# A transposed copy of x at the opening, and gate and up weights in one array laid out by chunk and row

## The reference

```
x = x + 0.5 * SwiGLU_1(rmsnorm(x, ffn1_norm))
x = x + token_mixing(rmsnorm(x, mix_norm), ...)     # three attentions on one projection, gated, then w_out
x = x + 0.5 * SwiGLU_2(rmsnorm(x, ffn2_norm))
rmsnorm(x, g) = x * rsqrt(mean(x * x) + 1e-6) * g
swiglu(x)     = (silu(x @ w_gate) * (x @ w_up)) @ w_down      # 1024 -> 2816 -> 1024
```

## Time and profile before

| | |
|---|---|
| time, median of 3 runs | 1138.39 us (1137.74 to 1138.44) |
| time of the profiled execution | 1138.71 us |
| its span, first to last instruction | 1136.9 us |
| TensorE busy | 1133.1 us of the span |
| VectorE / ScalarE / GpSimd busy | 770.4 / 630.6 / 70.3 us |
| read from memory | 205.29 MB, 181 GB/s over the span |

### The profile page before, as it was taken

The page is one execution under the profiler, slowest core; times in us unless marked ns, Lnnn a source line. Parts: engine busy times, 40 slices in busy tenths (PEclk is TensorE's granted clock), DMA queues, the critical chain, the costliest instruction groups (busy, mean ns, idle before and its releaser), DMA issues.

```text
span 1136.9 us, 16092 instructions
## 1 busy us (share of the span) xinstructions
PE 1133.1 (100%) x5975; PEld 966.9 (85%) x5975; DVE 770.4 (68%) x1055; ACT 630.6 (55%) x941; POOL 70.3 (6%) x79
## 2 busy tenths in 40 slices
PE   9999999999999999999999999999999999999999
PEld 7888888888888888888888888888887888888887
DVE  5766666868768676655766856678676695766655
ACT  6644445666674564544564544466766745544542
POOL 3020000202000000000020200002110000000000
PEclk9999999999999999999999999999999999999999
DMA  9956654545544666656566555636445445656521
GB/s 324 319 175 198 187 192 140 185 136 198 148 148 152 219 223 187 193 177 219 172 169 228 185 185 186 200 98 220 148 163 172 182 154 183 222 185 202 193 86 37
DMA packets 138828, 207.34 MB, mean 182 GB/s; under 512 B 6898, under 2 KB 99876, under 8 KB 138756
## 3 DMA queue, kind: packets, MB, share of 16 engines
q1 hardware_dynamic: 137364, 205.02, 55.1%
q0 software_dynamic: 752, 0.79, 0.8%
q10 hardware_dynamic: 640, 0.55, 0.2%
HBM read 205.29 MB, written 1.05 MB: 181 GB/s over the span
## 4 chain that ended last, share of the span: by engine, by line
PE 100%; DVE 0%; issue 0%; POOL 0%; DVEq 0%; POOLq 0%
PE bank L560 28%; PE bank L530 17%; PE bank L534 17%; PE bank L533 17%; PE bank L564 15%; PE bank L546 1%; PE bank L859 1%; PE bank L849 1%; PE bank L830 1%; PE bank L668 1%; PE bank L848 1%; PE bank L877 1%; PE bank L569 0%; PE bank L738 0%; PE bank L735 0%; PE bank L732 0%
## 5 line engine op out<-in xcount | busy, mean ns | idle before, releaser
L1300 DVE TENSOR_TENSOR w_low<-raw,w_high 128x1024 fp32r<-128x1024 f32 x388 | 464.2, 1232 | 281.4 <-ACT w_high L1016 280.8
L1016 ACT ACTIVATE w_high<-raw 128x1024 fp32r<-128x1024 f32 x387 | 393.5, 1055 | 317.8 <-PE bank L564 173.5
L560 PE MATMUL bank<-xT,w_high 128*128 128x512 f32 x1388 | 331.6, 390 | 0.1
L560 PEld LDWEIGHTS bank<-xT,w_high 128*128 128x128 f32 x1388 | 257.0, 188 | 51.2 <-DVE xT L1318 0.2
L564 PEld LDWEIGHTS bank<-xT,w_low 128*128 128x128 f32 x1408 | 175.7, 191 | 3.6
L564 PE MATMUL bank<-xT,w_low 128*128 128x256 f32 x1408 | 178.6, 283 | 0.0
L530 PE MATMUL bank<-w_high,xT 128*128 128x512 f32 (+1 forms) x440 | 171.3, 389 | 0.0
L534 PE MATMUL bank<-w_low,xT 128*128 128x512 f32 (+1 forms) x440 | 168.2, 382 | 0.0
L533 PE MATMUL bank<-w_high,xT 128*128 128x512 f32 (+1 forms) x440 | 168.1, 382 | 0.0
L530 PE MATMUL bank<-w_high,oT_high 128*128 128x512 f32 x418 | 162.6, 389 | 0.0
L534 PE MATMUL bank<-w_low,oT_high 128*128 128x512 f32 x418 | 162.2, 388 | 0.0
(11 more groups left out here) (146 smaller groups left out, 771.5 us busy)
## 6 DMA issues: line engine op xcount, KB each, us to landing
raw<-in_w_in SPq DMA_DIRECT2D x92, 512.0 KB, 4.6
raw<-in_ffn_w_down SPq DMA_DIRECT2D x88, 512.0 KB, 4.3
raw<-in_ffn_w_gate SPq DMA_DIRECT2D x86, 512.0 KB, 4.1
raw<-in_ffn_w_up SPq DMA_DIRECT2D x86, 512.0 KB, 5.0
raw<-in_w_out SPq DMA_DIRECT2D x16, 512.0 KB, 4.4
raw<-in_w_branch_c SPq DMA_DIRECT2D x8, 512.0 KB, 4.0
raw<-in_w_branch_a SPq DMA_DIRECT2D x4, 512.0 KB, 4.1
raw<-in_w_branch_b SPq DMA_DIRECT2D x4, 512.0 KB, 6.0
```

The lines of the kernel that those rows point to most:

```text
L560: return nc.tensor.matmul(bank[b0 + n][:, :], w_high[:, slot, column(k, n)], xT[:, k], start=k == 0, stop=full_last and k == KB - 1)
L1016: act.activation(w_high[:, slot], raw[:, in_slot, (p % 2) * 1024:(p % 2) * 1024 + 1024], ACT.Copy).then_inc(sem["high_ready"], 1)
L1300: dve.tensor_tensor(w_low[:, slot], raw[:, FILL_SLOT[p // 2], (p % 2) * 1024:(p % 2) * 1024 + 1024], w_high[:, slot].bitcast(F32), ALU.sub ...
```

## The change

Three things are changed together.

- The host hands in `x_turned`, x transposed to 1024x256. Five transfers bring it to SBUF in blocks of 128 features (1, 1, 2, 2, 2 blocks; rows of 1 KB per block). ACT and DVE make the high and low parts of the blocks from it, and the 16 transposes of x go. The squares are taken on ACT from `x_turned` (two times 128x1024), DVE sums them over the eight blocks with one `tensor_reduce` that reads 128x2048 elements in steps of 1 KB, and two float32 matmuls with a column of ones (`sum_squares`) sum over the partitions; ACT copies the two sums out, POOL's `norm` follows as before. `turn_row` moves from after 16 wide matmuls of chunk 2 to after 24 wide and 8 narrow ones; `sum_squares` stands where `cold_row` stood. x itself is loaded later, on POOL's queue, after the fourth hidden chunk; `trig` and the small parameters are loaded after the second one. In the cold start, the squares stand before `high(0, 4)` on ACT, and on DVE the reduce stands before `low(0, 4)`, and `low(0, 7)` before the scaling by the row.
- The gains come as one array `gains` with features in the partitions; the gain transposes (L978, L723) and the copies after them go. POOL scales the diff_subln column.
- Gate and up weights come as one array, laid out by chunk, half, row and block: a row of a block is 2 KB (256 gate and 256 up columns), and a fill's two transfers take two blocks each, 4 KB in one piece. For the first pairs each transfer is one block of 256 KB.

The warm-up becomes one run of 11 matmuls on a tile of ones. Pair 0 is cut by block: DVE copies the high half of block 0 itself, ACT that of block 1.

```diff
-            load_x(0)
-            load_x(1)
-            first_rows(sp, 1, fill_landed[FILL_SLOT[0]])
-            load_x(2)
-            first_rows(sp, 2, first_landed[2])
-            first_rows(sp, 3, fill_landed[FILL_SLOT[1]])
+            load_x_turned(0)
+            load_x_turned(1)
+            load_x_turned(2)
+            first_rows(sp, 2, 2, fill_landed[FILL_SLOT[0]])
+            load_x_turned(3)
+            first_rows(sp, 4, 2, third_landed)
+            load_x_turned(4)
+            first_rows(sp, 6, 2, fill_landed[FILL_SLOT[1]])
...
+                    v = slot.rearrange("p (k c) -> p k c", k=4)
+                    for k in (0, 2):
+                        yield v[:, k:k + 2], w[bass.ds(layer, 1), bass.ds(c, 1), k0 // 4, :, k:k + 2].rearrange("o n p k c -> p (o n k) c")
...
+            def sum_squares():
+                pe.wait_ge(sem["up_summed"], 1)
+                pe.wait_ge(block_squares_summed, 1)
+                for half in range(HALVES):
+                    last = nc.tensor.matmul(bank[4][:, half:half + 1], block_sums[:, half * P:half * P + P], ones[:, 0:1].bitcast(F32),
+                                            start=True, stop=True)
+                last.then_inc(squares_summed, 1)
...
                     if opens and not turned:
-                        cold_row()
+                        sum_squares()
                     gate_up_wide(layer, p + 2, 2, done + 1, i * 12)
                     gate_up_narrow(layer, p, 0, done + 1, i * 12).then_inc(sem["pair_used"], 1)
+                    if opens and not turned:
+                        turn_row(0, 1, 4)
...
-            warm(WARM_FIRST)
+            warm(WARM)
             pe.wait_ge(ident_ready, 1)
-            pe.wait_ge(first_gains_loaded, 16)
-            nc.tensor.transpose(bank[3][:, 0:16], gain_rows[0:16, :], ident[0:16, 0:16]).then_inc(first_gains_turned, 1)
-            warm(WARM_SECOND)
...
+                act.wait_ge(gains_loaded, 16)
+                act.wait_ge(x_turned_landed[0], 16)
+                block(0).then_inc(block0_high, 1)
+                act.wait_ge(x_turned_landed[1], 16)
+                block(1).then_inc(sem["blocks_high"], 1)
+                high(0, 0)
+                for p in range(1, 4):
+                    act.wait_ge(x_turned_landed[p + 1], 16)
+                    block(2 * p)
+                    block(2 * p + 1).then_inc(sem["blocks_high"], 1)
+                    high(0, p)
+                for first in (0, D):
+                    last = act.activation(x_squares[:, first:first + D], x_turned[:, first:first + D], ACT.Square)
+                last.then_inc(block_squares_ready, 1)
                 high(0, 4)
-                act.wait_ge(x_loaded[2], 16 * HALVES)
-                squares()
...
+                dve.wait_ge(half_landed[0], 16)
+                dve.tensor_copy(w_high[:, slot, 0:512], raw[:, in_slot, 0:512]).then_inc(half_high, 1)
+                dve.drain()
+                half_of_low(slice(0, 512)).then_inc(half_low, 1)
...
                 p = 4
+                dve.wait_ge(block_squares_ready, 1)
+                dve.tensor_reduce(block_sums, x_squares.rearrange("p (k s) -> p s k", k=KB), axis=AXIS_X, op=ALU.add).then_inc(block_squares_summed, 1)
                 low(0, p)
                 low(0, p + 1)
                 sum_gate(0, 1)
                 sum_up(0, 1)
                 low(0, p + 2)
+                low(0, p + 3)
                 dve.wait_ge(sem["row_ready"], 1)
```

More of the change, by code:

```diff
@@ L220, in build, with first_rows @@
         block = ctx.enter_context(nc.Block())
[L222 to L227, removed]
+        def first_rows(engine, k0, nk, landed):
+            v = raw[:, FILL_SLOT[k0 // 4]].rearrange("p (k c) -> p k c", k=4)
+            for k in range(k0, k0 + nk):
+                engine.dma_start(v[:, k % 4], a["ffn1_gate_up"][0, 0, k // 4, :, k % 4]).then_inc(landed, 16)
         def qk_blocks(first, count):
@@ L667, in warm @@
                 for _ in range(count):
-                    nc.tensor.matmul(bank[7][:, :].rearrange("p (a b) -> p a b", a=4), zero[:, :],
-                                     zero[:, :].unsqueeze(1).to_broadcast([P, 4, P]), start=True, stop=True)
+                    nc.tensor.matmul(bank[7][:, :].rearrange("p (a b) -> p a b", a=4), ones[:, :],
+                                     ones[:, :].unsqueeze(1).to_broadcast([P, 4, P]), start=True, stop=True)
             def cold_chunk():
                 b0 = inner_bank(1)
[L675 to L680, removed]
                 full, high_part, low_part = inner_parts(PAIR_SLOT[0], b0)
-                pe.wait_ge(sem["blocks_high"], 1)
+                pe.wait_ge(block0_high, 1)
                 pe.wait_ge(half_high, 1)
@@ L685, in cold_chunk @@
                     high_part(0, n, w_high, True)
+                pe.wait_ge(half_low, 1)
+                for n in range(4):
+                    high_part(0, n)
+                pe.wait_ge(block0_low, 1)
+                for n in range(4):
+                    low_part(0, n)
+                pe.wait_ge(sem["blocks_high"], 1)
                 pe.wait_ge(sem["high_ready"], value("high_ready", 0, 1))
@@ L1121, in ffn_chunks @@
                 if not cold:
[L1122 removed]
+                    act.activation(sink_exp_of[0][:, 0:1], ones[:, 0:1].bitcast(F32), ACT.Silu)
                     act.drain()
@@ L1642, in _ @@
             dve.sem_inc(sem["low_ready"], CREDIT["low_ready"])
-            dve.wait_ge(first_gains_ready, 1)
-            dve.wait_ge(lam_init_ready, 1)
             for layer in range(DEPTH):
                 if layer == 0:
-                    for p in range(4):
-                        blocks_low(layer, ST_FFN1, p // 2, G_FFN1, (p % 2,))
-                        low(layer, p)
+                    cold_pairs()
                 else:
@@ L1680, in rotary_constants, with gate_up_rows, gain_columns @@
     return np.ascontiguousarray(table.reshape(2, HALVES, P, DH).transpose(2, 0, 1, 3).astype(np.float32))
+def gate_up_rows(gate, up):
+    both = np.stack([gate, up], axis=2).reshape(DEPTH, 2, 4, P, 2, CHUNKS, FC)
+    return np.ascontiguousarray(both.transpose(0, 5, 1, 3, 2, 4, 6).reshape(DEPTH, CHUNKS, 2, P, 4, 2 * FC))
+def gain_columns(inputs):
+    columns = [inputs[name].reshape(DEPTH, KB, P).transpose(2, 0, 1) for name in ("ffn1_norm", "mix_norm", "ffn2_norm")]
+    columns.append(inputs["diff_subln"].reshape(DEPTH, 1, P).transpose(2, 0, 1))
+    columns.append(np.broadcast_to(np.asarray(LAM_INIT, np.float32).reshape(1, DEPTH, 1), (P, DEPTH, 1)))
+    return np.ascontiguousarray(np.concatenate(columns, axis=2).astype(np.float32))
 def kernel(**inputs):
```

172 lines of the change are left out of this document (87 added, 85 removed).

## The result

| | before | after |
|---|---|---|
| median | 1138.38 us (1137.58 to 1138.78, 22 runs) | 1139.70 us (1139.19 to 1140.14, 22 runs) |
| profiled execution, span | 1138.71, 1136.9 us | 1139.23, 1137.4 us |

The changed kernel takes 1.0012 times as long, with an interval of 1.0007 to 1.0018: 1.3 us more.

A forecast was written before the change was run, and what follows sets the result against it. TensorE's own list was taken to bound the kernel (busy 1133.1 of 1136.9 us). An earlier start and dropped transposes, less new waits, gave -1.25 us: 1138.39 - 1.25 = 1137.1 us, range 1135.2 to 1139.4.

The forecast's parts named there:

- the reduce reads 2048 elements in steps of 1 KB [...] I take 2.3: DVE's sum of squares ahead of `sum_up`, priced at 2.3 us from contiguous rows of 1.06 ns an element.
- The other end, 4.6: Upper price in us kept for DVE's reduce, twice the contiguous 2.3.
- the strided reduce: Rival: DVE's reduce ahead of `sum_up` dearer than 2.3 us; at twice that 1139.4 us; chance 0.10 for over 1.5 times.
- the predicted 31.35: Start of the down product in chunk 1, in us, against 32.59 before: 1.25 us earlier.
- No PE wait afterwards: Behind the first down matmul, near 31.4 us, TensorE would wait for nothing more.
- The start of the work: First real matmul, pair 0, would come at 5.95 us instead of 8.13, range 5.3 to 6.2.
- The low clock: Pair 0: matmuls from 5.95 to 6.8 us run at half rate, costing 0.43 us.
- The cover is spent by the move of the row: First down product: moved `turn_row` leaves fewer matmuls over the 5.85 us chain to `hidden_low`; TensorE waits 1.2 us.
- To spare 1.2: Before `turn_row`: ACT's copy and POOL's part hidden by 2.8 us of matmuls, with 1.2 us to spare.
- the landing at 12.92: Last weights of chunk 1, predicted to be issued at 6.44 us and landed 6.5 later, at 12.95.
- the layout's price of nothing: Larger weight rows claimed to be worth nothing past the opening, as no PE wait is put down to a transfer.
- the later loads of x and the constants: Loads of x, `trig` and parameters on POOL's queue, claimed to cost nothing; about 6.5 us once if cover were missing.

The follow-up runs named there:

- `layout_only`: Kernel before with only the gate and up weights read from the new array, opening as it was: 1138.71 us, 1.0002 of before.
- the five executions above: Single profiled executions of the changed kernel and four variants of it; last weights of chunk 1 landed at 12.92 to 13.45 us, executions took 1139.23 to 1139.76 us.
- `warm3`: Changed kernel with 3 warm-up matmuls in place of 11: 1139.62 us, 1.0010 of before.
- `row_early`: Changed kernel with `turn_row` ahead of the eight narrow matmuls, right behind the third group of wide ones: 1139.70 us, 1.0013 of before.
- `row_filled`: Changed kernel with high 8, high 9 (ACT) and low 8, low 9 (DVE) ahead of the row; strided reduce stays: 1138.80 us, 1.0004 of before.
- `tree_filled`: `row_filled` with three contiguous additions in place of the strided reduce as well: 1137.56 us, 0.9992 of before.
- `old_fills`: Changed kernel with weight fills past the first four pairs read from the old arrays in rows of 1 KB: 1139.56 us, 1.0010 of before.

## Why the prediction was wrong

**The step that failed** is "the reduce reads 2048 elements in steps of 1 KB [...] I take 2.3". It measured 3.90, 1.7 times the contiguous price. The other end, 4.6, was kept, and the rival "the strided reduce" gave 1139.4 for it: the right mechanism with the right place, at a chance of 0.10. That 1139.4 lies so near the measured 1139.70 is luck, though: by the rival's own sum the measured 3.90 makes 1138.7. I chose by the nearest row, which was a row of another access; nearest in kind it wasn't. The Trainium skill, page "SBUF — State Buffer", section "Door 1: The DMA port swizzle", says that each access that crosses to a new 16-byte line pays a penalty. The runs agree: 3.90 in steps of 1 KB, 2.29 in order.

**From the predicted 31.35 for the first down matmul to 32.96,** step by step:

| stretch | predicted | measured | difference |
|---|---|---|---|
| to the reduce (weights land 12.95; squares) | 16.05 | 15.93 | -0.12 |
| the reduce | 2.3 | 3.90 | +1.60 |
| from its end to `sum_squares` | 3.65 | 3.53 | -0.12 |
| sums, 16 matmuls, `turn_row` | 3.45 | 3.73 | +0.28 |
| from the turn to the end of `hidden_low` | 5.85 | 5.82 | -0.03 |

So the chain was right but for one term; the 0.28 is what a restart costs (the sums 0.61 and the first wide eight 1.95, for 0.43 and 1.84). At 31.35 the first down matmul would have ended at 31.85, against 33.21 before: a gain of 1.36, where I had 1.25 by comparing weight loads, of which before's ran ahead of its matmul. 1.61 later that is a loss of 0.25, as chunk 3's start shows (0.27).

**"No PE wait afterwards" was wrong.** DVE's backlog reaches `sum_up` of chunk 2 and costs 0.21 more. I had followed each wait to the next one on TensorE and not what DVE still owed. Together +0.48, the profiled pair's difference. The median lies another 0.8 off: I took it to be 0.3 below the profiled execution, as before's is, and it is 0.5 above. Both halves come from times of one execution that I took for fixed. The start at 8.13 is 7.46 in `layout_only`. And the chain now begins with a landing, which took 6.50 to 6.87 us from its issue in the five executions above. Of the 2.6 us between my 1137.1 and 1139.70 the reduce is thus 1.6, DVE's debt 0.2 and the place of the profiled executions 0.8; the first alone would have left the time within the range.

**The start of the work.** First real matmul predicted 5.95 (5.3 to 6.2), measured 6.35: block 0 landed at 5.78, not 5.28, with DVE's copy at 0.43, not 0.65. Pair 1 predicted at 9.4, 9.95 measured; chunk 2 at 17.8, 18.4 measured. The low clock was priced at 0.43 and cost nothing here, since the matmuls of the warm-up fell to 390 ns, those of the 2.4 GHz level, from about 4.1 us on already, not from 6.8 as in the earlier trace rows:

```profile
L676 PE MATMUL bank<-ones x3: 390/397/537, 3.7 to 4.3; 128*128 128x512 f32 x3
```

It ended earlier too, and TensorE stood 1.2 us for the weights. None of these sizes matters, as `warm3` shows with a start of chunk 2 later by a whole microsecond.

**"The cover is spent by the move of the row"** was the smaller part of the reason for a right number. The wait for `hidden_low` is 1.2 as predicted, and so is the 5.82 us chain behind the turn; but `row_early` undoes the move in part and gains 0.1 on this stretch, and `row_filled` and `tree_filled` leave the row where the change put it and have no such wait. The cause is the serial chain, in which ACT and DVE stand idle ahead of the row for 2.94 and 2.03 us, as the changed kernel's timeline has it in brackets:

```profile
27.12 0.39 ACT L1101 ACTIVATE norm_row<-bank 128x256 f32<-128x256 f32 x1 [2.94 <-PE bank L669]
...
27.60 0.69 DVE L1391 TENSOR_TENSOR work<-work,norm_row 128x512 f32<-128x512 f32 x1 [2.03 <-ACT norm_row L1101]
```

`row_filled` takes 0.9 off by filling these gaps.

**"To spare 1.2"** over POOL's norm was in truth 0.36: its first operation took 1.19 beside DVE, for 0.19 without. The row was ready at 26.50, and TensorE came to it at 26.86.

**Right:** the landing at 12.92 in this execution, the squares at 1.99, the layout's price of nothing (`layout_only`, `old_fills`), and the later loads of x and the constants, which nobody waits for.

## What to carry to other kernels

A matmul list shortened in an opening pays only if the chain of the other engines ends earlier too: follow that chain from its last transfer, and give a strided access its own price (here 1.7 times the contiguous one), or use whole contiguous additions. Where TensorE has slack, ask which engine owes most (here DVE) and fill its idle gaps; a wait that is moved by reordering comes back where that engine is needed next. A chain that begins with a transfer takes over that transfer's scatter between executions. And before a prediction leans on a time from one profiled execution, such as the start of real work, ask whether another execution of the same order has it elsewhere.

## What the runs showed of the hardware

**Strides.** DVE's reduce of 2048 float32 elements took 2.29 us in order and 3.90 to 3.92 in steps of 1 KB, some 0.8 ns more for each element. ACT's write of 1024 elements took 2.2 us in steps of 32 bytes and 1.0 in order.

**POOL beside DVE.** A POOL operation on 128x2 elements took 0.19 us with DVE idle, 1.17 to 1.19 beside low parts that DVE ran back to back, and in `row_filled` 3.46:

```profile
23.56 4.62 DVE L1301 TENSOR_TENSOR w_low<-raw,w_high 128x1024 fp32r<-128x1024 f32 x4
...
24.77 3.46 POOL L468 TENSOR_SCALAR small<-small 128x2 f32<-128x2 f32 x1 [20.88 <-ACT small L1092]
...
29.16 0.43 PE L669 MATMUL bank<-ident,small 128*128 128x128 f32 x2 [0.42 <-POOL small L470]
```

It ends at 28.23, 0.05 after DVE's run of four; in `tree_filled`, with the same run of four beside it, the same operation took 1.17. The Trainium skill, page "SBUF — State Buffer", section "Who interferes with whom", says that a DVE instruction with two SBUF inputs, as these are, contends with a GpSimd instruction that reads SBUF, as this one does. The runs agree, and in this execution POOL stood through more than one instruction of DVE.

**The clock after a wait.** In that execution of `row_filled` TensorE had stood 1.7 us at `sum_squares`. The windows behind it (us; PE, PEld, DVE, ACT, POOL busy; granted clock; DMA share, GB/s):

```profile
24.00:26.00 2.00, 2.00 (x9) 1.67 (x9) 2.00 (x3) 1.13 (x2) 1.23 (x1) 0.76 1.01 399
26.00:28.00 2.00, 2.00 (x8) 1.71 (x8) 2.00 (x2) 0.00 (x0) 2.00 (x1) 0.50 1.04 416
```

The granted clock was down to 0.50, the 1.2 GHz level, and this execution took 1.5 us more than the kernel's median. The trace puts that to POOL and not to the clock: the slowed TensorE came to the row's turn at 28.74 and stood there 0.42 more for POOL, which ended at 29.11, and by the 24 narrow matmuls behind the turn (2.87 us, as the earlier trace rows has 3.83 for 32) the clock was back. The waits of 1.1 and 1.2 us in the changed kernel, of 1.4 in `row_early` and of 1.5 in `old_fills` were followed by no such fall in their profiled executions; what decides it isn't shown.
